# Grouped-query attention: a pair's twenty transposes of probabilities in one run, behind four fifths of its projection work

## The reference, cut to what matters

```
def gqa_attend(q, k, v):
    s = einsum('bqhgd,bkhd->bhgqk', q, k) * (64 ** -0.5)
    p = softmax(s, axis=-1)
    return einsum('bhgqk,bkhd->bqhgd', p, v)

o  = gqa_attend(rope(rms_norm(q)), k_all, v_all)     # tokens see context and tokens
y  = (o * silu(g)) @ w_out ;   x = x + gate * y
oc = gqa_attend(rms_norm(qc), kc, vc)                # context sees only the context
```

## Time and profile before

| | |
|---|---|
| median of three runs | 3584.6 us |
| the profiled execution | 3585.31 us, with a span of 3583.5 us |
| PE busy | 3411.1 us (95%) |
| DVE busy | 1646.0 us (46%) |
| ACT busy | 1145.2 us (32%) |
| GpSimd (POOL) busy | 506.0 us (14%) |

### The profile page before, as it was taken

One profiled execution on the slowest core, in us unless ns is written; L12 is line 12 of the kernel. 1 busy time (PEld: TensorE's weight loads), 2 busy tenths in 40 slices (PEclk: granted clock), 3 DMA queues, 4 the chain that ended last, 5 costly groups with the idle time before them and its releaser, 6 DMA issues.

```text
span 3583.5 us, 54359 instructions
## 1 busy us (share of the span) xinstructions
PE 3411.1 (95%) x22927; PEld 1934.7 (54%) x22927; DVE 1646.0 (46%) x2612; ACT 1145.2 (32%) x1927; POOL 506.0 (14%) x489
## 2 busy tenths in 40 slices
PE   8999999998899989899999999989999999899999
PEld 4466555654333334445655555655555666466654
DVE  2555666634211138235555444552225565455632
ACT  1334343311111124333333333342214444244430
POOL 0222222311100014011101001001111000200000
PEclk9999999999999999999999999999999999999999
DMA  3022211214899899100000000031100000000001
GB/s 115 25 66 72 66 38 53 91 58 148 341 343 384 295 390 349 37 18 18 2 17 19 18 19 12 1 133 59 37 0 12 1 1 14 24 1 1 1 27 68
DMA packets 115386, 302.57 MB, mean 84 GB/s; under 512 B 13142, under 2 KB 55446, under 8 KB 101958
## 3 DMA queue, kind: packets, MB, share of 16 engines
q1 hardware_dynamic: 78470, 231.86, 17.9%
q10 hardware_dynamic: 29760, 42.05, 3.2%
q0 software_dynamic: 6912, 25.17, 1.9%
HBM read 345.67 MB, written 55.10 MB: 112 GB/s over the span
## 4 chain that ended last, share of the span: by engine, by line
PE 86%; DVE 7%; ACT 2%; DMA 2%; issue 2%; POOL 1%; SPq 1%; POOLq 0%; DVEq 0%; ACTq 0%
PE ps L2838 11%; PE ps L452 9%; PE ps L2284 8%; PE ps L2313 8%; PE ps L3550 7%; PE ps L1845 6%; PE ps L2856 5%; PE ps L3822 3%; PE ps L3231 3%; PE ps L1269 3%; PE ps L1865 3%; PE ps L3503 2%; PE ps L2522 2%; PE ps L3220 1%; PE ps L3211 1%
## 5 line engine op out<-in xcount | busy, mean ns | idle before, releaser
L2838 PE MATMUL ps<-sb 128*128 128x512 f32 x960 | 464.5, 603 | 19.6 <-ACT sb L2196 10.9
L2284 PEld LDWEIGHTS ps<-sb 128*128 128x128 f32 x2624 | 288.1, 141 | 303.8 <-ACT sb L2292 129.9
L2284 PE MATMUL ps<-sb 128*128 128x128 f32 x2624 | 417.3, 282 | 19.4 <-ACT sb L2292 9.5
L2292 ACT ACTIVATE sb<-ps 128x512 f32<-128x512 f32 x336 | 200.2, 597 | 714.6 <-PE ps L2284 714.6
L2258 ACT ACTIVATE sb<-ps,sb 128x1280 f32<-128x1280 f32 (+1 forms) x288 | 353.5, 1232 | 130.4 <-DVE sb L2251 111.9
L2300 DVE COPY sb<-ps 128x512 f32<-128x512 f32 x320 | 220.2, 689 | 376.0 <-PE ps L2284 375.6
L452 PE MATMUL ps<-sb 128*128 128x512 f32 x704 | 348.2, 615 | 5.1 <-DMA sb<-in_w_in 3.5
L3550 PE MATMUL ps<-sb 96*128 96x512 f32 (+1 forms) x768 | 332.7, 526 | 8.7 <-DVE sb L3607 7.2
L2313 PEld LDWEIGHTS ps<-sb 128*64 128x64 f32 x5248 | 287.6, 138 | 70.7 <-issue 40.4
L2313 PE MATMUL ps<-sb 128*64 128x128 f32 x5248 | 322.2, 277 | 3.3 <-DVE sb L2300 3.1
L2079 POOL TENSOR_TENSOR sb<-sb 128x1 f32<-128x1 f32 (+3 forms) x114 | 132.1, 1159 | 1058.4 <-DVE sb L2075 1058.3
(11 more groups left out here) (376 smaller groups left out, 4336.6 us busy)
## 6 DMA issues: line engine op xcount, KB each, us to landing
sb<-in_exp_gate SPq DMA_DIRECT2D x65, 1024.0 KB
sb<-in_exp_up SPq DMA_DIRECT2D x65, 1024.0 KB
sb<-in_exp_down SPq DMA_DIRECT2D x65, 1024.0 KB
sb<-in_l_w_mod ACTq DMA_DIRECT2D x12, 2048.0 KB, 15.6
d_ys<-sb ACTq DMA_DIRECT2D x32, 512.0 KB, 4.2
d_ys<-sb SPq DMA_DIRECT2D x64, 256.0 KB
sb<-d_x SPq DMA_DIRECT2D x32, 512.0 KB, 3.8
sb<-in_w_in SPq DMA_DIRECT2D x22, 512.0 KB, 4.7
```

The costliest lines, as they stand in the source:

```text
L2284: ins = k.pe.e.transpose(k.bank(bank)[:, 128 * j:128 * j + 128], self.Pb[g % 2][:, 1280 * b + 128 * c:1280 * b + 128 * c + 128], k.f(C_ID, ...
L2292: k.act.e.activation(self.PT[:, xs[0]:xs[-1] + 1, :], k.bank(bank)[:, 0:128 * len(xs)].rearrange("p (j t) -> p j t", j=len(xs)), ACT.Copy) ...
L2838: ins = pe.e.matmul(k.bank(5), lhs[:, kk, :], w[:, kk, 512 * half:512 * half + 512], start=kk == 0, stop=kk == 7)
```

## The change

In pairs 0 to 71 the order of a period becomes: score of g, weigh of g-1, the projection steps of places 0 to 3, all five groups of transposes of g itself, and the steps of place 4 (in a context pair: place 0, the one group, place 1). So a pair is turned in its own period instead of in the one after. The exponentials move one place forward, after places 0 and 1. The five groups go to banks 6, 0, 1, 3 and 4; the last four are score banks that the exponentials have emptied. ACT copies groups 0, 2 and 4, DVE 1 and 3. A score now also waits for all copies of the pair before it. Pairs 72 to 79 and the second attention layer keep the order of before.

```
+        if g < self.together:
+            return (6, 0, 1, 3, 4)[u]
...
+        if bank in (5, 6):
+            k.pe.wait_ge(*(k.free[5] if bank == 5 else self.free6))
+        elif bank > 1:
+            k.pe.wait_ge(*self.t["exp", g, 1])
...
+    st.together = len(st.pairs) - 8
...
+    def in_turn(p):
+        return 4 if p > 2 else 1
...
+        for g in range(st.together):
...
+            yield ("score", g)
+            if g:
+                yield ("weigh", g - 1)
+                if (g - 1) % 4 == 3:
+                    yield ("consume", st.pairs[g - 1][0], (g - 1) // 4 % 2, g - 1)
+            for u in range(places(g)):
+                if u == in_turn(places(g)):
+                    for v in range(st.parts(g)):
+                        yield ("pturn", g, v)
+                if place < len(todo):
+                    yield from todo[place]
+                place += 1
+                if u == max(exp_at(g, 0) - 1, 0):
+                    yield ("exp", g, 0)
+                if u == max(exp_at(g, 1) - 1, 0):
+                    yield ("exp", g, 1)
+                    if p == 0:
+                        yield ("silu", n)
...
+        for name in ("pt_a", "pt_v"):
+            pe.wait_ge(*st.t.get(name, FREE))
...
-        elif kind == "pturn" and x[1] < 2:
+        elif kind == "pturn" and (x[1] % 2 == 0 if x[0] < st.together else x[1] < 2):
```

More of the change, by code:

```diff
@@ L2227, in __init__ @@
         self.p_free, self.pt_free, self.free6, self.free7 = [FREE, FREE], FREE, FREE, FREE
+        self.together = 0
     def cols(self, g, b):
@@ L2266, in parts, with turn_bank @@
         return (2 * self.pairs[g][2] + 3) // 4
-    def turn_bank(self, u, other):
+    def turn_bank(self, g, u, other):
+        if g < self.together:
+            return (6, 0, 1, 3, 4)[u]
         return 5 if other and u % 2 else 6
@@ L2274, in turned_out @@
             self.k.free[5] = token
-        else:
+        elif b == 6:
             self.free6 = token
     def pe_turn(self, g, u, other=False):
-        k, nk, bank = self.k, self.pairs[g][2], self.turn_bank(u, other)
-        k.pe.wait_ge(*(k.free[5] if bank == 5 else self.free6))
+        k, nk, bank = self.k, self.pairs[g][2], self.turn_bank(g, u, other)
+        if bank in (5, 6):
+            k.pe.wait_ge(*(k.free[5] if bank == 5 else self.free6))
+        elif bank > 1:
+            k.pe.wait_ge(*self.t["exp", g, 1])
         for j, x in enumerate(self.part(g, u)):
@@ L2288, in act_turn @@
     def act_turn(self, g, u, other=False):
-        k, xs, bank = self.k, self.part(g, u), self.turn_bank(u, other)
+        k, xs, bank = self.k, self.part(g, u), self.turn_bank(g, u, other)
         k.act.wait_ge(*self.t["turn"])
@@ L2798, in everything @@
         todo, place = [], 0
-        for g in range(-1, G + 1):
+        for g in range(st.together):
+            n, p, _ = st.pairs[g]
+            if p == 0:
+                starts = list(itertools.accumulate((places(x) for x in range(g, g + 8)), initial=0))
+                todo, place = dealt(window(n), starts[-1], starts), 0
+            yield ("score", g)
[14 more added lines that the diff above has]
+                    yield ("exp", g, 1)
+                    if p == 0:
+                        yield ("silu", n)
+        for g in range(st.together - 1, G + 1):
             if g + 1 < G:
@@ L2805, in everything @@
                 yield ("score", g + 1)
-            if g > 0:
+            if g >= st.together:
                 yield ("weigh", g - 1)
@@ L2811, in everything @@
                 for u in range(places(g)):
-                    if g >= 0 and u < st.parts(g):
+                    if g >= st.together and u < st.parts(g):
                         yield ("pturn", g, u, n + 1 == NTT and place >= len(todo))
@@ L2958, in dve_program @@
             st.dve_max(*x)
-        elif kind == "pturn" and x[1] > 1:
+        elif kind == "pturn" and (x[1] % 2 if x[0] < st.together else x[1] > 1):
             st.dve_turn(*x)
```

## The result

The changed kernel takes **3628.2 us** (median of four runs, 3623.1 to 3630.1), the kernel before 3581.3 beside it: a ratio of 1.0123, with an interval of 1.0107 to 1.0139. The forecast was 3618, slower, with a range of 3601 to 3640. Beside the experiments the kernel before had medians of 3579.7 (seven runs) and 3582.8 (twelve), from 3577.3 to 3592.2.

What follows compares the result with a forecast made beforehand. PE was taken to bound the kernel, so only its gaps could be won. Tiles 3 to 8 +16.5, tile 2 +3.3, end -2, context +7.4 and clock +8.5 made +33.7 us: 3618 from 3584.6, range 3601 to 3640.

Steps and rivals of the forecast that it cites:

- The first pair: First pair of a token tile: products wait for turne behind the silu, 17.95 us instead of 15.17, +2.8.
- the bound that the prediction named: First pair of a token tile: 16.5 us without the silu ahead, the lower bound of that item.
- One of its signs: Start of tile 1: the first mmq should start 12 us after score 0 instead of 6.8.
- The pairs 1 to 7: Rest of a token tile: pairs 42, 43, 47 together -0.3 us, 44 -0.6, 45 +0.1, 41 -0.1, 46 +0.85.
- The clock: A fall at each token tile's start, three more in tiles 3 to 8, plus tile 2 and pair 1: +8.5 us.
- The context: Context pairs: transposes and first products wait for ACT, mainly in pairs 0, 1, 8 and 9: +7.4 us, bounds 4 and 10.
- repeat it: Context pairs 8 and 9: the same waits as pairs 0 and 1, with more work in front, 3.2 us.
- Tile 2 and the end: Tile 2: 110.2 us instead of 106.87, +3.3; pairs 72 and 73: -2, between 0 and -2.7.
- Faster: Rival, token tiles: bank 5's copies stay hidden and the first pair stays at 15.17 us; -23, 3562; chance 0.03.
- About the same: Rival, token tiles: first pair only 16.5 us and no new fall of the clock; 3593 us; chance 0.08.
- The chain shows in every pair: Rival, 56 token pairs: DVE or ACT late by 0.5 us in each, 28 more, 3647; chance 0.10.
- Transposes count as idle: Rival, 56 pairs: each run costs a fall of the clock, 1.7 us each, 95 more, 3713; chance 0.02.

Runs made afterwards that it cites:

- The kernel with bank 6 alone: The changed kernel with all five groups of transposes through bank 6 instead of banks 6, 0, 1, 3 and 4: 3985.5 us, ratio 1.1115.
- the kernel with filler: The changed kernel with unread products in PE's three waits for bank 5 in each token tile's first pair: 3613.0 us, ratio 1.009.
- the context alone with the wait in all pairs: The changed kernel with only the 16 context pairs in the new order, every score still waiting for the copies: 3622.4 us, ratio 1.0112.
- the version placed by hand: Against the kernel before: token pairs' runs of twenty placed where bank 5 changes hands, turnh, qturn, silu and output products moved, context unchanged: 3568.3 us, ratio 0.9959.

## Why the prediction was right, and short by a quarter

**The mechanism and the sign were right.** The first pair of a tile hangs on score, reduction, exponentials, load, silu, `turne`, products, as the row of the 2.80 wait shows, with the products at 11.87 us instead of 12.1. Moving the silu alone gives back 14 to 16 us, and leaves a first pair of 16.5 at full clock, the bound that the prediction named. One of its signs came out larger: the first `mmq` of tile 1 started 13.1 us after score 0 (1477.75 - 1464.62), not 12. And in a tile's first pair the run did not have the full clock that was forecast for it, since the fall began ahead of it.

**The pairs 1 to 7, forecast -0.05 a tile, were +0.55.** Pairs 42, 43, 44 and 47 came as forecast to 0.03. Pairs 41, 45 and 46 each took 0.17 to 0.26 more than my sums (12.76, 13.27, 12.75 against 12.5, 13.1, 12.55). In all three a copy out of bank 5 has no group of transposes beside it any more. Pair 46 shows the slip (PE in the changed kernel):

```profile
2021.90 3.70 PE L2871 MATMUL ps<-sb 128*128 128x512 f32 x8
2026.48 0.63 PE L2929 MATMUL ps<-sb 128*128 128x128 f32 x4 [0.88 <-DVE sb L3069]
```

The next transposes start 4.58 us after the products, not 3.5 + 0.88: the idle time of 0.88 begins where the last pass ends (2025.60), and that lies 0.2 behind the slot in which the next instruction would have been issued. I had added an idle time to a start-to-start price. (The terms listed for pair 46 also add up to 12.6, not 12.55.) The kernel with bank 6 alone has the same (idle 0.69, start 0.85 later). Over six tiles the pairs 1 to 7 are 3.7 of the missing 10.9.

**The first pair, forecast +2.8 at full clock, was +2.5** (17.68 in the kernel with filler, against 15.17): 1.6 too much in six tiles, the other way.

**The clock, forecast 1.7 a fall, was 2.2.** The number of falls in tiles 3 to 8 was right, all six instead of three. The size was taken from the earlier trace rows, where a fall lasts 3.4 us; behind the longer wait it lasts 6.8, of which 2.3 are idle and cost nothing. That is 3 us in tiles 3 to 8. The granted clock never fell beside a run of twenty that stood behind full work. The Trainium skill ("TensorE: Matmul & The Clock Gate", Part 4: PE-mode transpose) says that transpose mode does not count as PE-busy in the same way. The trace does not show it to matter here: with the waits filled the clock stays at 1.00 over 110.49 us with eight runs in them, and the row was the better guide.

**The context, forecast +7.4 and one fall, was +13.6.** This is the term that was mis-sized most, 4.5 of the 10.9. Pairs 0 and 1 cost 7.3 against 5.6. Pairs 8 and 9 "repeat it", said the prediction, and took 3.2 because more work lies in front; they cost 5.5 (6.52 and 15.97 against 3.80 and 13.17), because the waits there, 1.85 and 3.47 us, come with more of the slow clock, which I had not counted there: 13.6 us at half the clock in two falls, where the kernel before has one of 3.4. At pairs 0 and 1 the one fall that I had counted lasts 10.2 us. The rest is +0.7 and +0.6 in pairs 4 and 12, 0.05 in each plain pair, and -0.4 in pairs 11 and 15.

**Tile 2 and the end.** +6.1 against +5.0, and -2.1 against -2. The fall at tile 2's start lasts 10.2 us now and 6.8 before. Pair 72 took 8.11 instead of the forecast 8.15, and score 73 waits 5.1 us for the exponentials, which is the chain that bounds it.

**The rivals.** "Faster" needed the first pair under 15.5: it took 17.7 without any fall. "About the same" needed a first pair of 16.5 and no new fall, and neither came; its sum also takes 12 off for a first pair at 16.5, where 1.45 in each of seven tiles is 10. "The chain shows in every pair" had its sign in pairs 1 to 7 but not its size, 0.1 a pair instead of 0.5. "Transposes count as idle" needed a fall in each of 56 pairs; the changed kernel has one in each first pair alone, and none with the waits filled.

**What the prediction did not see** is that the wait added to every score is a cost of its own: put into the kernel before, it alone takes 24 us. It was priced only where it shows in the new order (0.4 and 0.85), which happened to be enough there (6.6 us in seven tiles).

**What stays open.** The changed kernels' medians lie above what their attention stages explain by 0 to 9 us (most for the context alone with the wait in all pairs, 42.6 against 33.7). The executions of before spread over 15 us themselves, and no experiment was made on this. The filler replaces idle time and leaves the transposes, so it shows that the falls need the waits; whether the transposes between the waits help to bring them was not separated.

## What to carry to other kernels

Moving transposes out of the gaps of a one-buffer chain into a block wins 0.1 us where the period was full (0.6 in pair 44, where the groups had to wait for their own bank), but takes the filler out of the chain; look first at what stands between two uses of the scarce bank once the block is gone. A run belongs beside the longest wait, not behind it (the version placed by hand did this, among other things), and a start-to-start price and an idle time must not be added without the tail between them. And a wait that is harmless in the new order should be priced in the old one too, since a partial roll-back meets it.

## What the runs showed of the hardware

- Waits are paid twice when they cluster. Of three waits of 0.88, 1.46 and 2.80 us at a tile's start, the third saw a fall to 1.2 GHz begin that lasted 6.8 us and cost 2.2; four waits of 0.69 to 0.79 between short groups of transposes brought a fall too, within or right behind them, in 49 of 49 pairs. Five products at a tile's start (2.74 us for the last three) kept 2.4 GHz and saved 15.8 us in seven tiles, though nothing reads them.
- A run of twenty float32 transposes takes 2.35 us (pair 46), and the full clock holds through it and in the whole of the filled tile with eight of them.
- A handoff of one PSUM bank between PE and a copying engine delays the next group by more than PE's idle time in the trace: 0.85 to 1.0 us against 0.69 to 0.79.
